# Retention's gate projection by a seven-product block scheme in place of eight, its weight sums formed on VectorE

## The reference, cut to what matters

```python
q, k, v, g = jnp.split(h @ w_in, [R_QK_COLS, 2 * R_QK_COLS, 2 * R_QK_COLS + R_V_COLS], axis=-1)
...
s = jnp.einsum('bhqd,bhkd->bhqk', qi, ki) * intra
o = jnp.einsum('bhqk,bhkv->bhqv', s, vi) + jnp.einsum('bhqd,bhdv->bhqv', qi, state) * q_dec
...
o = (of * lax.rsqrt(jnp.mean(of * of, axis=-1, keepdims=True) + EPS)).astype(dt)
return (jax.nn.silu(g) * o.reshape(B, S, R_V_COLS)) @ w_o
```

## Time and profile before

| what | value |
|---|---|
| time, median of 3 runs (lowest, highest) | 1263.24 us (1262.98, 1263.55) |
| span of the profiled execution | 1261.0 us |
| the profiled execution's own time | not listed apart from the runs; the median stands 2.2 us above the span |
| busy: PE, PEld, DVE, ACT, POOL | 1256.3, 1037.7, 723.1, 464.9, 151.8 us |
| retention on PE | about 499 to 898 us of the span |

### The profile page before, as it was taken

The page is one execution under the profiler, slowest core; times in us unless marked ns, Lnnn a source line. Parts: engine busy times, 40 slices in busy tenths (PEclk is TensorE's granted clock), DMA queues, the critical chain, the costliest instruction groups (busy, mean ns, idle before and its releaser), DMA issues.

```text
span 1261.0 us, 15536 instructions
## 1 busy us (share of the span) xinstructions
PE 1256.3 (100%) x5831; PEld 1037.7 (82%) x5831; DVE 723.1 (57%) x929; ACT 464.9 (37%) x655; POOL 151.8 (12%) x138
## 2 busy tenths in 40 slices
PE   9999999999999999999999999999999999999999
PEld 8777888888888888888888888888888888888887
DVE  6776686666663333546535634744786667763222
ACT  6664454444442222232232223233454444442120
POOL 3751400000000011403102202201000000000000
PEclk9999999999999999999999999999999999999999
DMA  6202222222222224321312221221232222222222
GB/s 245 68 34 92 84 101 100 100 100 100 100 69 92 92 91 155 127 78 72 127 67 75 100 100 67 109 83 52 101 109 100 100 100 90 84 77 98 103 91 89
DMA packets 22030, 120.44 MB, mean 96 GB/s; under 512 B 2692, under 2 KB 3976, under 8 KB 11240
## 3 DMA queue, kind: packets, MB, share of 16 engines
q1 hardware_dynamic: 21048, 117.61, 26.8%
q10 hardware_dynamic: 720, 1.97, 0.4%
q0 software_dynamic: 224, 0.35, 0.1%
HBM read 117.81 MB, written 2.11 MB: 95 GB/s over the span
## 4 chain that ended last, share of the span: by engine, by line
PE 98%; DVE 1%; DMA 0%; POOL 0%; ACT 0%; issue 0%; DVEq 0%
PE ps L1355 32%; PE ps L1357 32%; PE ps L1356 32%; PE ps L1408 1%; PE ps L1505 1%; PE ps L1492 1%; PE ps L1483 1%; DVE w_lo L681 0%; DMA gain_x<-in_x_first 0%; PE ps L1466 0%; PE ps L1372 0%; DVE mx L803 0%; POOL qs L1245 0%; DVE qss L775 0%; PE ps L1394 0%; PE ps L1456 0%
## 5 line engine op out<-in xcount | busy, mean ns | idle before, releaser
L1355 PE MATMUL ps<-h_hi,w_hi 128*128 128x512 f32 x960 | 375.9, 392 | 0.0
L1357 PE MATMUL ps<-h_hi,w_lo 128*128 128x512 f32 x960 | 374.1, 390 | 0.0
L1356 PE MATMUL ps<-h_lo,w_hi 128*128 128x512 f32 x960 | 374.1, 390 | 0.0
L681 DVE TENSOR_TENSOR w_lo<-raw,w_hi 128x2048 fp32r<-128x2048 f32 (+1 forms) x115 | 244.4, 2125 | 143.2 <-ACT w_hi L364 143.2
L364 ACT ACTIVATE w_hi<-raw 128x2048 fp32r<-128x2048 f32 (+1 forms) x115 | 202.6, 1761 | 189.2 <-PE ps L1357 189.2
L1357 PEld LDWEIGHTS ps<-h_hi,w_lo 128*128 128x128 f32 x960 | 180.3, 188 | 37.6
L1355 PEld LDWEIGHTS ps<-h_hi,w_hi 128*128 128x128 f32 x960 | 180.4, 188 | 37.2
L1356 PEld LDWEIGHTS ps<-h_lo,w_hi 128*128 128x128 f32 x960 | 180.4, 188 | 36.4
L1356 PE MATMUL ps<-g_lo,w_hi 128*128 128x512 f32 x352 | 137.1, 390 | 0.0
L1355 PE MATMUL ps<-g_hi,w_hi 128*128 128x512 f32 x352 | 137.1, 390 | 0.0
L1357 PE MATMUL ps<-g_hi,w_lo 128*128 128x512 f32 x352 | 137.1, 390 | 0.0
(11 more groups left out here) (185 smaller groups left out, 1453.4 us busy)
## 6 DMA issues: line engine op xcount, KB each, us to landing
raw<-in_w_up SPq DMA_DIRECT2D x44, 1024.0 KB, 4.8
raw<-in_w_ret SPq DMA_DIRECT2D x32, 1024.0 KB, 4.8
raw<-in_w_dn SPq DMA_DIRECT2D x32, 704.0 KB, 4.0
raw<-in_w_ao SPq DMA_DIRECT2D x4, 1024.0 KB, 4.9
raw<-in_w_q SPq DMA_DIRECT2D x3, 1024.0 KB, 5.1
gain_x<-in_xT SPq DMA_DIRECT2D x7, 256.0 KB, 4.8
out<-gain_x SPq DMA_DIRECT2D x7, 256.0 KB, 5.3
rbc<-root_mem SPq DMA_DIRECT2D x6, 256.0 KB, 3.0
```

Source lines behind the costliest of these rows:

```text
L681: nc.vector.tensor_tensor(w_lo[:, s, 0:cols], raw[:, s, 0:cols], w_hi[:, s, 0:cols].bitcast(F32), ALU.subtract).then_inc(w_lo_ok, 1)
L1355: nc.tensor.matmul(dst, st[0], mv[0], start=start, stop=False)
L1356: nc.tensor.matmul(dst, st[0], mv[1], start=False, stop=False)
L1357: return nc.tensor.matmul(dst, st[1], mv[0], start=False, stop=stop)
```

## The change

The 2x2 block product of a gate unit (two tiles of 128 gates, two halves of the input features, two halves of the positions) is made of seven block products of 256 positions (84 matmuls in place of 48 of 512 positions). The weight blocks are quarters (`quad`, 128x512) of a unit. After the seven products some block sums are left in PSUM, others are added in `sg` by copies on ACT (`copy_c11`, `copy_lower`, `copy_c12`) and by additions on DVE (`add_c11`, `add_c12`, `sub_lower`).

Sums of weight blocks are formed in `raw` by DVE: one (`sum_first`) before the unit is split, three after; three quarters are then split again (`mid_hi` on ACT, `mid_lo` on DVE) once their first products are done. So `raw[:, s]` of a gate unit comes free only after the last `mid_lo`, and the next load into it waits for that (`load_after_gates`). Four sums of blocks of the hidden state (`tT_hi`, `tT_lo`) are formed once, in head 0 (`turned`, `turned_lo`, `turned_hi`), and their `f32` form borrows `sg` and `pf`.

```diff
+            def load_after_gates(src, pair, s, h):
+                sp.wait_ge(mlo_ok, 3 * gate_unit(h, s) + 3)
+                sp.dma_start(raw[:, s, :], src).then_inc(w_loaded[s], 16)
...
+            def split_summed(n, pair, s):
+                act.wait_ge(sum_ok, 4 * n + 1)
+                split(pair, s, UW)
+
+            def mid_hi(n, s, i):
+                act.wait_ge(prod_done, 6 * n + i + 1)
+                act.wait_ge(sum_ok, 4 * n + i + 2)
+                nc.scalar.activation(w_hi[:, s, quad(i)], raw[:, s, quad(i)], ACT.Copy).then_inc(mhi_ok, 1)
...
+            def split_summed(n, pair, s):
+                split(pair, s, UW)
+                dve.wait_ge(w_lo_ok, 2 * pair + s + 1)
+                nc.vector.tensor_tensor(raw[:, s, quad(0)], raw[:, s, quad(0)], raw[:, s, quad(2)],
+                                        ALU.add).then_inc(sum_ok, 1)
...
             def qkvg(h, first, final=False):
                 p0 = PAIR_RET if first else PAIR_RET + 4 * h - 1
...
                 rotated_lo(h, 1)
-                if not first:
+                if first:
+                    turned(0)
+                    turned(1)
+                    turned_lo(0)
+                    turned(2)
+                    turned_lo(1)
+                    turned(3)
+                    turned_lo(2)
+                    turned_lo(3)
+                else:
...
-                split(pv + 1, 0, UW)
+                sum_first(n0, pv + 1, 0)
+                split_summed(n0, pv + 1, 0)
+                sum_first(n1, pv + 1, 1)
...
-                split(pv + 1, 1, UW)
...
+                gate_in(0)
+                sub_lower(n0, pv + 1, 0, c0, 4)
+                gate_in(1)
+                split_summed(n1, pv + 1, 1)
                 split(pv + 2, 0, UW)
+                mid_lo(n1, 1, 0)
+                add_c11(n1, c1, 6)
+                mid_lo(n1, 1, 1)
+                if not final:
+                    cross_sums(CROSS_HEAD + h, SQ_HEAD + 4 * h + 4)
+                mid_lo(n1, 1, 2)
...
+            def upper_products(n, s, bank):
+                product(left(bank), s, 0, pure(0, 0), True).then_inc(prod_done, 1)
+                product(right(bank), s, 1, pure(0, KT // 2), False).then_inc(prod_done, 1)
+                product(right(bank + 1), s, 2, turned(T1), True).then_inc(prod_done, 1)
+                product(left(bank + 1), s, 3, turned(T4), False, 0, 2)
...
+                if first:
+                    pe.wait_ge(tlo_ok, 4)
+                pe.wait_ge(vlo_ok, 4 * h + 2)
+                upper_products(n0, 0, 4)
+                fourth_end(0, 4)
+                lower_products(n0, 0, 4)
+                seventh(0, 4, 0, KT // 2).then_inc(w_used, 1)
...
-                    gate_part(2, 0, KT).then_inc(g_done, 1)
-                    pe.wait_ge(gx_ok, 4 * h + 2)
                     pe.wait_ge(part_ok, CROSS_HEAD + h + 1)
-                    gate_part(3, 0, 1)
+                    fourth_end(1, 6)
                     cross_columns(bank=4)
-                    gate_part(3, 1, 6)
+                    lower_products(n1, 1, 6)
+                    seventh(1, 6, 0, 1)
                     pe.wait_ge(r_ok, ST_HEAD + h + 1)
-                    gate_part(3, 6, 7)
+                    seventh(1, 6, 1, 2)
                     cross_row(bank=5)
-                    gate_part(3, 7, KT).then_inc(w_used, 1)
+                    seventh(1, 6, 2, KT // 2).then_inc(w_used, 1)
```

More of the change, by code:

```diff
@@ L55 @@
 WARM_MMS = 4
+HALF = S // 2
+QUAD = UW // 4
+T1, T4, T2, T3 = range(4)
 GAINS = 4 * KT
@@ L337, in _ @@
             spread(ROW_R, 0, crossed=False)
-            for j in range(2, 4):
-                for s in range(2):
-                    load(w_ret[2 * j + s], PAIR_RET + j, s, UW)
+            for s in range(2):
+                load(w_ret[4 + s], PAIR_RET + 2, s, UW)
+            for s in range(2):
+                load_after_gates(w_ret[6 + s], PAIR_RET + 3, s, 0)
             with sp.Fori(0, R_HEADS - 1) as h:
@@ L617, in qkvg @@
                     nc.scalar.activation(p_hi[:, t, 0:w], pf[:, t % 2, 0:w], ACT.Copy).then_inc(phi_ok, 1)
+                probs_hi(0)
+                probs_hi(1)
+                mid_hi(n0, 0, 0)
+                copy_c11(n0, c0, 4)
+                probs_hi(2)
+                mid_hi(n0, 0, 1)
+                probs_hi(3)
+                mid_hi(n0, 0, 2)
+                copy_lower(n0, c0, 4)
+                copy_c12(n0, c0, 4)
                 for m in range(2):
@@ L623, in qkvg @@
                     square(SQ_HEAD + 4 * h, m, ps[:, m, :])
-                gate(h, 2)
+                mid_hi(n1, 1, 0)
+                copy_c11(n1, c1, 6)
+                mid_hi(n1, 1, 1)
+                mid_hi(n1, 1, 2)
+                copy_lower(n1, c1, 6)
                 if final:
+                    copy_c12(n1, c1, 6)
                     broadcast_out(1, bank=5)
@@ L628, in qkvg @@
                         out_hi(h, m)
+                    gate(h, 2)
                     gate(h, 3)
@@ new lines, in mid_lo, with add_c11 @@
+            def mid_lo(n, s, i):
+                dve.wait_ge(mhi_ok, 3 * n + i + 1)
+                nc.vector.tensor_tensor(w_lo[:, s, quad(i)], raw[:, s, quad(i)], w_hi[:, s, quad(i)].bitcast(F32),
+                                        ALU.subtract).then_inc(mlo_ok, 1)
+            def add_c11(n, c, bank):
+                dve.wait_ge(ac_ok, 3 * n + 1)
+                nc.vector.tensor_tensor(c[:, 0, 0:HALF], ps[:, bank, 0:HALF], c[:, 0, 0:HALF],
+                                        ALU.add).then_inc(cd_ok, 1)
@@ L1066, in qkvg @@
                                             ALU.mult).then_inc(pf_ok, 1)
+                p_part(0)
+                p_part(1)
+                p_lo_part(0)
+                p_part(2)
+                mid_lo(n0, 0, 0)
+                add_c11(n0, c0, 4)
+                p_lo_part(1)
+                p_part(3)
+                mid_lo(n0, 0, 1)
                 p_lo_part(2)
+                mid_lo(n0, 0, 2)
                 p_lo_part(3)
+                add_c12(n0, c0, 4)
                 def gate_in(m):
-                    nc.vector.tensor_tensor(sg[:, m, :], ps[:, 4 + m, :], rbc[:, 0, :], ALU.mult).then_inc(gx_ok, 1)
+                    dve.wait_ge(cd_ok, 3 * gate_unit(h, m // 2) + 2 + m % 2)
+                    nc.vector.tensor_tensor(sg[:, m, :], sg[:, m, :], rbc[:, 0, :], ALU.mult).then_inc(gx_ok, 1)
                 def normalised(m):
```

193 lines of the change are left out of this document (154 added, 39 removed).

## The result

The changed kernel takes 1276.38 us (median of 4 runs, 1274.89 to 1277.11) against 1263.31 beside it (1262.98 to 1263.55): ratio 1.0102, 95% interval 1.0088 to 1.0117. It is 13.1 us slower where 6.8 were forecast; the sign was right, and the time lies 0.4 us above the range. The profiled execution took 1274.89 us with a span of 1272.8, 11.8 more than the 1261.0 before. Two executions that took far longer than all the others, 4465 us in the kernel with the early sums and 1556 us in the one with PE's new order, are left out of all that follows.

What follows compares the result with a forecast made beforehand. PE was taken as the bound, busy 1256.3 of 1261.0 us. Terms +4.6 (head 0), -2.9 (first halves), +3.1 (second halves), +2.0 (last head) gave +6.8: span 1267.8, median 1270.0, range 1266 to 1276.

Steps and rivals of the forecast that it cites:

- The waits and their places: PE stands 5.6 us before head 0's first gate unit, 2.0 in heads 0 to 2's second units, 3 before last `project`.
- Four scalings: Head 0, new DVE work ahead of `v_lo`: scalings of 256 columns at 0.40 each; by the skill's rule 0.5 us less.
- floor of 1.55: Heads 0 to 2, second half: least time PE waits for `cross_sums`, without turns between POOL and DVE.
- the 2.0 taken: Heads 0 to 2, second half: PE's wait for `cross_sums` with turns between POOL and DVE, 2.0 us.
- T: Start of a head's second gate unit, from which the second half's times were counted.
- T + 4.65: Heads 0 to 2: end of the second `mid_lo`, behind which DVE reaches `cross_sums`, counted from T.
- Turns between POOL and DVE: Second half: POOL's additions and DVE's remainder take turns, so the sums are there at T + 7.0 instead of T + 6.5.
- The loads: Two 1 MB loads go out ahead of the inverse root's spreading; delaying it 2.4 leaves 0.9 us, costed at nothing.
- The price of a product: Gate units: 84 matmuls at 0.118 us make 9.95 in place of 10.94, 0.98 less per unit.
- a rival with chance 0.27: Head 0: clock falls to 1.2 GHz after PE's wait, costing 0 to 5.7 us, middle 2.8, giving 1272.8; chance 0.27.
- one sentence on the later waits: Within the clock rival: the later waits of 2 to 3 us may also make the clock fall; no size given.
- a late spreading: Rival: spreading delayed 4 us or more, PE waits 1 us or more for k units, heads 1 to 3; 1273 to 1276; chance 0.10.

Runs made afterwards that it cites:

- early sums: Changed kernel with three of the four sums of hidden blocks moved ahead of the first rotation of head 0; 1269.97 us, ratio 1.0056.
- PE's new order: Changed kernel with PE's wait for `cross_sums` behind the fifth product, row turned in the next head's first tile, last head's columns and broadcast earlier; 1272.48 us.
- filled waits: Idle matmuls put into PE's waits: head 0's in the changed kernel, 1272.59 us; all others in the kernel with early sums, 1266.64 us.
- late split: Seven products in first gate units, eight in second, early sums, DVE's split of the second unit behind `add_c12`; 1267.51 us, ratio 1.0033.
- earlier spreading: Seven products everywhere, early sums, PE's new order; SP issues the inverse root's spreading ahead of the next unit's load; 1264.36 us, ratio 1.0011.

## Why the prediction was right, and where it was wrong

- **The waits and their places: right.** Head 0: 5.0 us for `v_lo` where 5.6 was forecast. Four scalings took 1.14 us in place of 1.6 (0.28 each, where 256 columns of a tensor_tensor step by 0.34); the subtractions took 1.67 for four, 0.40 each and 0.07 for the end, as forecast. For the scalings the trace bears out the estimate that was worked out from the Trainium skill, "VectorE: DVE Perf Modes", section "The perf-mode tier table", by which they cost 0.5 us less and the wait was 5.1. Heads 0 to 2: 1.64 against a floor of 1.55 and the 2.0 taken. PE was released at T + 6.9 (7.0 forecast) but came 0.26 later than forecast, at T + 5.24, so that the wait was shorter and the matmuls ahead of it longer; that the half took 12.62 against 12.56, where the clock didn't fall, is in part two errors that cancel. (The terms given for T + 4.65 add up to 4.59, which moves nothing.) Last head: PE broadcast at 882.63, T + 9.6, DVE's normalising 1.72 later at 884.35, `project` at T + 14.92 against 14.6. The run with early sums takes the first wait away, that with PE's new order the second, and the halves then take 10.13 and 10.25.
- **Turns between POOL and DVE: right**, 4.24 and 3.38 us above.
- **The loads: right in the changed kernel, and near.** In head 1 the spreading took 6.2 us from the row to `rbc` (685.04 to 691.26), where before it took 4.4: 1.8 of the 3.3 us of room went, where 2.4 was the case worked out. DVE stood 4.11 us for it (3.01 in the earlier trace rows), and the split behind it ended at 694.95, 1.5 ahead of PE's need. In head 0 it took 2.8 us more than before (7.1 against 4.3), and nearly nothing was left. Without the other waits it is the next one.
- **The price of a product: right in kind, 0.18 us a unit too low.** 10.13 in place of 9.95: the step is 0.12 and not 0.118, which was read from the six matmuls of the earlier trace rows (and 84 x 0.118 is 9.91, not 9.95).
- **The step that failed: the clock, left out of the sum.** The sum took every matmul at 1.00, and the fall stood as a rival with chance 0.27, priced for head 0 alone (middle 2.8, measured 2.8; that the middle of 0 to 5.7 hit it is luck), with one sentence on the later waits. The prediction had named the clock leaving 1.00 as a sign that it is wrong, and this came true. What the runs showed: PE standing 4.0, 4.9 and 5.0 us in three kernels, and each time the clock fell; 2.87 us, a fall in two of three traces (1.5 us each); 1.64 us in the second halves, a fall in one of three heads in each of three traces (some 1.35 us); 1.4 to 1.64 us in seven other places, no fall; 1.02 us once, a fall; filled waits, none. In the changed kernel that is 2.8 in head 0 and 1.3 in head 2, and 1.5 more in most runs if the last `project` is what differs. "TensorE: Matmul & The Clock Gate", section "Part 1: The HAM clock gate", in the Trainium skill, says that an idle PE loses its clock. The traces agree for the three waits of 4.0 us and more; behind the shorter ones the clock fell in only some places.

The account of the profiled run against the forecast of 1267.8: clock 2.8 and 1.3, price of the products in the first halves 0.7, the rest of the second halves 0.3, head 1's q and k units, the `project` behind them and the last `project` 0.7, head 0's wait 0.6 less, start 0.2 less: the 5.0 us that are missing. This execution took 1274.89, within the range. The median lies 1.5 above it, and for those 1.5 us there is no trace. The range's upper end, 1276, held one fall of the clock and part of a late spreading; the runs had two falls, and perhaps a third, on top of the price.

What is shown: the clock's fall in head 0 (filled against not), the first wait's cause, the second wait's cause, and that seven products pay when nothing waits (first halves 10.13 for 10.94). What stays open: why a wait of 1.64 us makes the clock fall in one head and not in another of the same run, and where three of the four executions of the changed kernel lose 1.4 to 2.1 us more than the profiled one.

## What to carry to other kernels

Price a stall of PE with what comes after it: here a wait of 5 us cost 7.8 and one of 2.9 up to 4.4, and a wait where PE has never stood before has no row to read that from, so it belongs in the sum. A change that saves columns and puts steps on an engine's queue pays only once each reader of that queue has been looked up: moving statements in the queues, with the arithmetic unchanged, and leaving on the old scheme the one unit that no order tried here could hide turned +13.1 us into -4.7. When a wait is removed, name the next one first: two kernels here (PE's new order, the earlier spreading) gave part of their gain to a split that had had 1.5 us to spare in head 1 and hardly any in head 0, and more of it to the next split in the same queue.

## What the runs showed of the hardware that was not expected

- The fall isn't sure: behind 1.64 us of standing the clock went to 0.50 (of 2.4 GHz, so 1.2) in some heads and stayed at 1.00 in others of the same run; behind 1.02 us it fell once, in the kernel with the late split, and behind 1.43 us it didn't in three traces.
- It isn't at once: the six falls behind 1.02 to 2.87 us of standing began 0.8 to 1.5 us after PE had resumed, and each lasted about 3.4 us (0.57 over the 4.00 us from 780.00 in the changed kernel). Behind the 1.02 us it cost about 1.7, more than the wait.
- After 4.9 and 5.0 us of standing the clock was 0.50 from the first matmul, and back at 1.00 some 6 us later; after 4.0 us it was 0.50 for 3.4 us.
- Neither did 0.65 us of standing soon behind the start of the last `project` make it fall, in three traces.
